# Layer 0's scan: raw tiles in two PSUM banks, the transposes through the two others, a half product between them

## The chip, the cores and the metric

One core of one Trainium2 chip runs the whole model as one program. The metric is the device time of that program in microseconds. The program is written in single instructions: TensorE (PE) multiplies and writes to PSUM only, VectorE (DVE), ScalarE (ACT) and GpSimd (POOL) do everything between products, SyncE (SP) starts the loads of the weights. All data are fp32.

## The reference, cut to what matters

The model is a first transformer block and a second block of two layers. The change is in the second block's layer 0, in the part that is a Mamba-2 scan over 512 tokens (256 of the context, 256 of the latent). Each layer projects the normed input, sends part of the result (x, B and C) through a five-tap depthwise convolution and a SiLU, scans in both directions in chunks of 128 tokens, and gates the sum with a SiLU of z:

```
def dwconv_silu(x, w, bias):                       # kw = 5
    y = lax.conv_general_dilated(x, w[:, None, :], window_strides=(1,), padding=[(kw // 2, kw // 2)], ...)
    return jax.nn.silu(y + bias)

# ssd_chunked, per chunk of 128 tokens and group g of 8, 4 heads of 64 in each
chunk_states = jnp.einsum('bclgn,bclgr,bclgrp->bcgrpn', bc, decay_to_end, xc)
h = h * chunk_decay + chunk_states                 # from chunk to chunk
cb = jnp.einsum('bclgn,bcsgn->bclsg', cc, bc)
y = (jnp.einsum('bclsg,bclsgr,bcsgrp->bclgrp', cb, lmat, xc)
     + jnp.einsum('bclgn,bcgrpn,bclgr->bclgrp', cc, h_in, jnp.exp(cs)))

y = (yf + yb + ssd_d[:, None] * xs)
ssd = rmsnorm(y * jax.nn.silu(z), ssd_norm_g) @ w_ssd_o
```

The projections that feed it, `h @ w_in` (x, B, C and z of all eight groups) and the gate `gs`, are computed in the same stage.

## The kernel before, in words

The scan of layer 0 goes through eight groups `g`. Two kinds of work are interleaved by hand in it.

The first kind is the scan of group g. Its four convolved tiles (x in two, B, C; 128 channels by 512 tokens each) lie in `CV`. PE transposes the two x tiles and the B tile, four 128x128 transposes each (line 1512), ScalarE copies them out (`turned`, line 2031), PE makes the products C by B (line 1521, "the CB product"), which VectorE masks twice into `CBM` (line 2784). POOL scales x by its weights (`XD`, line 3165); PE makes from it and the transposed B the change of the state (line 1536, "the delta"); VectorE carries the state on (lines 2800 to 2806); PE multiplies the state by C (line 1553) and VectorE takes that to `Y` (lines 2826 to 2829). This goes three steps, i = 0, 1, 2. Then come four units: ScalarE makes decays (lines 2070, 2074), VectorE masks them (line 2839, `masked`), PE multiplies (line 1570, `within`). At the end VectorE adds all to Y (lines 2845 and 2851, `sum_y`), and one group later it multiplies by the gated z (line 2860, `times_z`).

The second kind is the projection of group g+1's x, B, C and of group g's z: one chunk of weights each (1024x256), three chunks to a group, `m = 3g, 3g+1, 3g+2`. Each chunk is multiplied by Winograd's form of the 2x2 block product, which takes seven half-size products (`pe_scan`, n = 0 to 6, each four matmuls of 256 columns, line 629; the trace counts each fp32 matmul twice) in place of eight. POOL prepares sums of the weights (lines 673 to 681). ScalarE keeps one product (`act_scan`, line 685). VectorE assembles the four results out of the banks PB (`dve_scan`, lines 693 to 705: U2, c11, U4, U3, c2, c21). PE may begin chunk m+1 only when VectorE has done U4 (line 697) of chunk m: this is the wait on `scan_free` in `pe_scan` for n = 0.

The assembled tiles of a chunk ("raw tiles", two of 128x512) go to `RAW_H`, an unused part of H in SBUF. ScalarE reads them for the middle tap and the bias (line 1990, `middle`), VectorE reads them for the four other taps (`raw_taps`, line 2738; source `RAW_H`, destination and second input the CV buffer in SBUF), and ScalarE reads z's raw tiles for the SiLU (line 2093). The CV buffer of layer 0 shows as X in the trace. In group 0 and in layer 1 the taps read a product straight from the PSUM banks PB instead (line 2771).

Of PSUM's eight banks four (PB) hold the seven products. The other four are PA[0], PA[1] (x tiles' transposes, then delta and the state's product, then `within`), PS[:,0] (B's transposes) and PS[:,1] (the CB product).

The order on PE is written by hand. `SCAN_FILL` says how many of the 21 half products go into each slot of a group: before, 2 behind the CB product, 2, 3, 2 behind the deltas of i = 0, 1, 2, then 2, 3, 2, 3 ahead of the four `within`, and 2 at the end. PE waits for `s_y` (the adds of `sum_y`) of the group before, at the head of a group. VectorE's order within a group: assemble(3g-1), the two masks of CB, times_z(g-1), the states of i = 0 and 1, assemble(3g), the rest of the states, masked(0), taps of tile 0, masked(1), taps of tile 1, assemble(3g+1), masked(2), taps of tile 2, masked(3), taps of tile 3, sum_y.

Of the kernel before, what the change touches and what calls it, by code (L numbers as in the profile page):

```python
# [9 lines left out]
P = 128  # L10
D = 1024
KT = D // P
T1 = 256
TT = 512
# [179 lines left out]
SCAN_EARLY = 4  # L194


SCAN_FILL = list(itertools.accumulate((2, 2, 3, 2, 2, 3, 2, 3, 2), initial=0))
assert SCAN_FILL[-1] == 21 and N_SCAN == 3 * SSD_GROUPS + 2


# [12 lines left out]
def program(nc, xT, stream, params, rows, consts, rel_bias, rev_hot, w_dt, scratch, cs_rows, x_kept, mrg_kept, out):  # L213
    ctx = ExitStack()
    with ctx:
# [732 lines left out]
        at += 1024  # L948
        assert at <= ARENA, at
        YT = [area(L_SSD + 2048 * i, 8, T1) for i in (2, 0, 3, 1)]  # L950
        RAW_H = H[:, 0:KT:2, T1:TT]
        SCAN_SUMS = [area(4096, 2, 4, 4, P), area(L_MRG, 2, 4, 4, P)]
        SCAN_KEEP, SCAN_U3 = par[:, 0:T1], c_("c_before")
        SCAN_U2, SCAN_U4 = (wdt[:, 0, 4 * i:4 * i + 4, :].rearrange("p k n -> p (k n)") for i in range(2))
# [123 lines left out]
        def _(pe):  # L1078
# [257 lines left out]
            for la in range(DEPTH_2):  # L1336
# [163 lines left out]
                def scan_group(g):  # L1500
                    b = g % 2
                    tok = [t for t in range(4) if live(la, t)]
                    if g >= 1:

                        pe.wait_ge(sem("s_y"), LAYER["s_y"] * la + 2 * g)
                    for i, bank in enumerate((PA[0], PA[1], PS[:, 0])):
                        if i == 2 and g == 0:
                            pe.wait_ge(sem("cs_turned"), la + 1)

                        pe.wait_ge(sem("s_conv"), LAYER["s_conv"] * la + 4 * g + i + 1)  # L1510
                        for t in range(4):
                            mm = pe.transpose(bank[:, t * P:(t + 1) * P], CV[b][:, i, t * P:(t + 1) * P], ident)
                        mm.then_inc(sem("s_turns"), 1)
                    pe.wait_ge(sem("s_conv"), LAYER["s_conv"] * la + 4 * g + 4)
                    if g == 0:

                        pe.wait_ge(sem("dt_rest"), LAYER["dt_rest"] * la + 2)
                    else:
                        pe.wait_ge(sem("s_cbm"), LAYER["s_cbm"] * la + 2 * g)
                    for t in tok:  # L1520
                        mm = pe.matmul(PS[:, 1, t * P:(t + 1) * P], CV[b][:, 2, t * P:(t + 1) * P],
                                       CV[b][:, 3, t * P:(t + 1) * P], start=True, stop=True)
                    mm.then_inc(sem("s_cb"), 1)
                    if la == 0:
                        fill(g, 0)
                    else:
                        project(g + 1, (0,))
                        if g + 1 == SSD_GROUPS:
                            project_z(g, (0,))

                    pe.wait_ge(sem("s_turned"), LAYER["s_turned"] * la + 3 * g + 3)
                    for i in range(3):
                        for d, order in enumerate((F_ORDER, B_ORDER)):
                            n = 6 * g + 2 * i + d
                            pe.wait_ge(sem("s_xd"), LAYER["s_xd"] * la + n + 1)
                            pe.matmul(PA[0][:, 256 * d:256 * d + 256], BT[:, order[i], :], XD[d],  # L1536
                                      start=True, stop=True).then_inc(sem("s_delta"), 1)
                        if la == 0:
                            fill(g, i + 1)
                        else:  # L1540
                            project(g + 1, ((1,), (2, 3), (4,))[i])
                            if g + 1 == SSD_GROUPS and i + 1 < T // P:
                                project_z(g, (i + 1,))

                        if i and inter_count(la, g, i - 1):
                            pe.wait_ge(sem("s_inter_read"), LAYER["s_inter_read"] * la + inter_count(la, g, i - 1))
                        for d, order in enumerate((F_ORDER, B_ORDER)):
                            n = 6 * g + 2 * i + d
                            pe.wait_ge(sem("s_state"), LAYER["s_state"] * la + n + 1)
                            t = order[i + 1]  # L1550
                            if live(la, t):
                                for q in range(2):
                                    mm = pe.matmul(PA[1][:, 256 * d + P * q:256 * d + P * q + P],  # L1553
                                                   HT[d][:, P * q:P * q + P], CV[b][:, 3, t * P:(t + 1) * P],
                                                   start=True, stop=True)
                                mm.then_inc(sem("s_inter"), 1)
# [17 lines left out]

                    if la == 0:
                        for u in range(len(units)):
                            fill(g, 4 + u)
                            within(u)
                        fill(g, 8)
                        return  # L1580
                    z_tiles = ((), (), (), (0,), (1,))
                    if g + 1 == SSD_GROUPS:
# [121 lines left out]
        def _(act):  # L1704
# [189 lines left out]
            for la in range(DEPTH_2):  # L1894
# [86 lines left out]
                def middle(g, chunks):  # L1981
                    b = g % 2
                    if la == 0 and 0 < g < SSD_GROUPS:
                        for j in chunks:
                            act.wait_ge(sem("scan_free"), 3 * (3 * (g - 1) + j) + 3)
                            if g >= 2 and j == 0:
                                act.wait_ge(sem("s_y"), 2 * (g - 1))
                            for t in range(2):
                                i, ch = 2 * j + t, channels(g, 2 * j + t)
                                copy(CV[b][:, i, :].rearrange("p (a n) -> p a n", a=2), RAW_H[:, 2 * t:2 * t + 2, :],  # L1990
                                     ACT.Identity, scale=par[:, W0 + 2 * 32 + ch:W0 + 2 * 32 + ch + 1],
                                     bias=par[:, CBs + ch:CBs + ch + 1]).then_inc(sem("s_mid"), 1)
                        return
                    for j in chunks if g < SSD_GROUPS else ():
# [24 lines left out]
                            act.wait_ge(evacuated[pair], 2 * before + i % 2 + 1)  # L2019
                        copy(CV[b][:, i, 0:Tc], CV[b][:, i, 0:Tc], ACT.Silu).then_inc(sem("s_conv"), 1)  # L2020

                def turned(g):

                    for i, bank in enumerate((PA[0], PA[1], PS[:, 0])):
                        act.wait_ge(sem("s_turns"), LAYER["s_turns"] * la + 3 * g + i + 1)
                        src = bank.rearrange("p (t n) -> p t n", t=4)
                        if i == 0 and g >= 1:

                            act.wait_ge(sem("s_xc"), LAYER["s_xc"] * la + 2 * len(units) * g)
                        dst = BT[:, :, :] if i == 2 else XG[:, :, i * P:(i + 1) * P]  # L2030
                        copy(dst, src, ACT.Copy).then_inc(sem("s_turned"), 1)  # L2031
# [55 lines left out]
                def silu_z(g):  # L2087
                    if la == 0:
# [1 line left out]
                        if g >= 1:  # L2090
                            act.wait_ge(sem("s_sum"), g)
                        for i in range(2):
                            copy(ZT[:, i, :].rearrange("p (a n) -> p a n", a=2), RAW_H[:, 2 * i:2 * i + 2, :], ACT.Silu)\
                                .then_inc(sem("s_silu"), 1)
                        return
                    pair, _ = GROUPS[f"z{la}"][g]
                    act.wait_ge(chunk_done, CHUNKS[f"z{la}"][g] + 1)
# [29 lines left out]
                if la == 0:  # L2127
# [1 line left out]
                        act.wait_ge(evacuated[pair], 2 * before + 2)  # L2129
                    act.dma_start(mrg_kept, MRG).then_inc(sem("kept_saved"), 16)  # L2130
                    for g in range(SSD_GROUPS):
                        turned(g)
                        if g:
                            silu_z(g - 1)
                        row_exps(g)
                        act_scan(act, 3 * g)
                        decay_exps(g, 0)
# [31 lines left out]
                def gates(j):  # L2169
                    if la == 0:  # L2170
                        act.wait_ge(sem("scan_free"), 3 * (N_SCAN - 4 + j) + 3)
                        for t in range(2):
                            gate = GS[:, 2 * j + t, :]
                            copy(gate.rearrange("p (a n) -> p a n", a=2),
                                 gate.rearrange("p (a n) -> p a n", a=2) if j else RAW_H[:, 2 * t:2 * t + 2, :],
                                 ACT.Sigmoid).then_inc(sem("gs_open"), 1)
                        return
                    pair, _ = GROUPS[f"gs{la}"][j]
                    act.wait_ge(chunk_done, CHUNKS[f"gs{la}"][j] + 1)
# [101 lines left out]
        def _(v):  # L2281
# [319 lines left out]
            for la in range(DEPTH_2):  # L2601
# [125 lines left out]
                def raw_taps(g, tiles):  # L2727


                    for i in tiles:  # L2730
                        v.wait_ge(sem("s_mid"), 4 * g + i + 1)
                        ch = channels(g, i)
                        for tap in (0, 1, 3, 4):
                            s_ = tap - 2
                            lo, hi = max(0, -s_), T1 - max(0, s_)
                            dst = CV[g % 2][:, i, :].rearrange("p (a b) -> p a b", a=2)[:, :, lo:hi]
                            src = RAW_H[:, 2 * (i % 2):2 * (i % 2) + 2, lo + s_:hi + s_]
                            ins = vec.scalar_tensor_tensor(dst, src, par[:, W0 + 32 * tap + ch:W0 + 32 * tap + ch + 1],  # L2738
                                                           dst, ALU.mult, ALU.add)
                            if tap == 4:  # L2740
# [4 lines left out]
                def assemble(m):  # L2745


                    tiles = RAW_H
                    if m >= N_SCAN - 3:
                        j = m - (N_SCAN - 4)  # L2750
                        tiles = GS[:, 2 * j:2 * j + 2, :].rearrange("p t (a n) -> p (t a) n", a=2)
                    dve_scan(v, m, tiles[:, 0, :], tiles[:, 1:4:2, :], tiles[:, 2, :])

                def taps(g, tiles):

# [22 lines left out]
                def states(g):  # L2778
                    if la == 0 and g >= 1:
                        assemble(3 * g - 1)  # L2780
                    v.wait_ge(sem("s_cb"), LAYER["s_cb"] * la + g + 1)
                    for d, tri in enumerate((c_("tri_le"), c_("tri_ge"))):
                        n = T // P
                        vec.tensor_tensor(CBM[:, d, tok, :], PS[:, 1, 0:T].rearrange("p (a b) -> p a b", a=n),
                                          tri.unsqueeze(1).broadcast_to([P, n, P]), ALU.mult)\
                            .then_inc(sem("s_cbm"), 1)
                    if g >= 1:
                        times_z(g - 1)
                    for i in range(3):
                        for d, order in enumerate((F_ORDER, B_ORDER)):  # L2790
# [562 lines left out]
```

## Time and profile before

| | us |
|---|---|
| median of three runs | 3018.41 |
| their lowest and highest | 3017.31, 3023.1 |
| the profiled execution's own time | 3029.04 |
| its span (first to last instruction) | 3027.2 |
| PE busy in it | 2938.1 (97%) |
| DVE busy | 1484.5 (49%) |
| ACT busy | 814.8 (27%) |
| POOL busy | 1036.3 (34%) |
| layer 0's scan, from its first transposes to its last `within` products | from 1121.3 to about 1540 of the span |

A row of the time line gives the start, the time from the first start to the last end of the instructions merged in it, the engine, the line, the operation, output and inputs, and how many (x); in brackets the idle time ahead of it and what ended that. A row by source line gives the shortest, median and longest duration in ns and the first and last start. DVE, at half the span busy, is only of interest where PE waits for it.

### The profile page before, as it was taken

Reading aid. Unit: us, or ns where it says so; the run is one execution under the profiler, and the core shown is the slowest. Engines: PE = TensorE matmul, PEld = TensorE weight load, DVE = VectorE, ACT = ScalarE, POOL = GpSimd, SP = SyncE. Lnnn points to the kernel's source line nnn. Section 1 sums busy time; section 2 is a strip of 40 time slices with the busy share of each in tenths; the row PEclk is TensorE's granted clock in tenths of the full one; section 3 lists DMA queues with packets and bytes.
Section 4 is the critical chain, followed back from the end, with each engine's and each line's share of the span. In section 5 each row is a group of like instructions: output and inputs, shape, how many; then the busy total and the mean of one; then the engine's idle time right before and its main releaser. Section 6 shows DMA issues by size and latency. Waiting matters only on the chain.

```text
span 3027.2 us, 40501 instructions
## 1 busy us (share of the span) xinstructions
PE 2938.1 (97%) x16088; PEld 2400.4 (79%) x16088; DVE 1484.5 (49%) x2765; ACT 814.8 (27%) x1778; POOL 1036.3 (34%) x876
## 2 busy tenths in 40 slices
PE   8999999999999999999999999999998999999999
PEld 7776799998855558887878788888886666678998
DVE  1243267813265638888763533342237555541651
ACT  1022222201022325665630110110104355540210
POOL 0000234574400115565654334443230111110686
PEclk9999999999999899999999999999999999999999
DMA  7455434442356033222232122222331323334443
GB/s 258 147 205 205 153 140 155 165 167 86 124 196 222 29 127 112 98 98 98 98 125 84 70 84 85 96 84 84 112 112 42 118 99 111 106 111 153 154 168 112
DMA packets 68977, 377.63 MB, mean 125 GB/s; under 512 B 6378, under 2 KB 24874, under 8 KB 26304
## 3 DMA queue, kind: packets, MB, share of 16 engines
q1 hardware_dynamic: 49120, 334.60, 30.6%
q10 hardware_dynamic: 18704, 36.90, 3.6%
q0 software_dynamic: 976, 3.63, 0.3%
q8 instruction: 127, 2.08, 0.3%
q14 instruction: 50, 0.41, 0.0%
HBM read 366.50 MB, written 4.42 MB: 123 GB/s over the span
## 4 chain that ended last, share of the span: by engine, by line
PE 60%; DVE 7%; ACT 1%; issue 1%; PEld 1%; POOL 0%; PEldq 0%; POOLq 0%; ACTq 0%; DVEq 0%
PE PB L501 12%; PE PB L629 8%; PE PA L501 7%; PE PB L1481 7%; PE PS L501 6%; PE PB L381 5%; PE PB L1188 2%; DVE X L2738 2%; PE PB L1454 2%; PE PB L425 2%; PE PA L1536 1%; PE PA L1570 1%; PE PA L1553 1%; ACT work L1945 1%; PE PB L1495 1%
## 5 line engine op out<-in xcount | busy, mean ns | idle before, releaser
L536 POOL TENSOR_TENSOR sums<-ring 128x512 f32<-128x512 f32 x115 | 150.6, 1309 | 603.4 <-PE PA L501 246.8
L501 PE MATMUL PB<-work,sums 128*128 128x128 f32 (+1 forms) x1360 | 230.5, 327 | 0.0
L1481 PE MATMUL PB<-H,ring 128*128 128x512 f32 (+1 forms) x576 | 229.5, 547 | 0.0
L501 PEld LDWEIGHTS PB<-work,sums 128*128 128x128 f32 x1360 | 207.0, 191 | 17.6
L501 PE MATMUL PA<-work,sums 128*128 128x128 f32 (+1 forms) x1280 | 208.9, 318 | 0.0
L734 DVE TENSOR_TENSOR work<-PA,work 128x128 f32<-128x128 f32 (+1 forms) x53 | 18.9, 357 | 381.4 <-ACT work L718 381.4
L501 PEld LDWEIGHTS PA<-work,sums 128*128 128x128 f32 x1280 | 187.4, 191 | 13.6
L3165 POOL TENSOR_TENSOR work<-work 128x256 f32<-128x256 f32 x96 | 59.7, 643 | 402.6 <-ACT work L2031 343.3
L1481 PEld LDWEIGHTS PB<-H,ring 128*128 128x128 f32 x576 | 109.0, 191 | 96.6 <-issue 92.2
L1188 PE MATMUL PB<-H,ring 128*128 128x256 f32 (+1 forms) x640 | 175.0, 428 | 0.4 <-DVE rstd L2381 0.2
L734 DVE TENSOR_TENSOR work<-PB,work 128x256 f32<-128x256 f32 (+1 forms) x34 | 13.0, 382 | 320.8 <-ACT work L718 320.8
L1188 PEld LDWEIGHTS PB<-H,ring 128*128 128x128 f32 x640 | 120.1, 192 | 46.3 <-issue 33.0
L541 POOL TENSOR_TENSOR sums<-ring,sums 128x512 f32<-128x512 f32 x115 | 151.9, 1321 | 9.0
L381 PE MATMUL PB<-work,ring 128*128 128x256 f32 (+1 forms) x544 | 152.7, 442 | 0.7 <-DVE work L2771 0.7
L539 POOL TENSOR_TENSOR sums<-sums,ring 128x512 f32<-128x512 f32 x115 | 149.6, 1301 | 0.0
L537 POOL TENSOR_TENSOR sums<-ring 128x512 f32<-128x512 f32 x115 | 149.0, 1296 | 0.0
L718 ACT ACTIVATE work<-PS 128x128 f32<-128x128 f32 (+1 forms) x53 | 17.5, 330 | 480.8 <-PE PA L501 433.8
L501 PE MATMUL PB<-work,ring 128*128 128x128 f32 (+1 forms) x840 | 143.5, 325 | 0.0
L629 PE MATMUL PB<-work 128*128 128x256 f32 x624 | 143.2, 382 | 0.0
L381 PEld LDWEIGHTS PB<-work,ring 128*128 128x128 f32 x544 | 103.2, 190 | 48.6 <-issue 38.4
L501 PEld LDWEIGHTS PB<-work,ring 128*128 128x128 f32 x840 | 127.0, 191 | 10.4
L501 PE MATMUL PS<-work,ring 128*128 128x128 f32 (+1 forms) x760 | 133.7, 319 | 0.0
(440 smaller groups left out, 6054.2 us busy)
## 6 DMA issues: line engine op xcount, KB each, us to landing
ring<-stream SPq DMA_DIRECT2D x314, 1024.0 KB, 4.8
sums<-cs_rows ACTq DMA_DIRECT2D x16, 1024.0 KB, 4.7
sums<-cs_rows ACTq DMA_DIRECT2D x16, 512.0 KB, 3.7
work<-work ACTq DMA_DIRECT2D x16, 256.0 KB, 4.8
work<-scratch POOLq DMA_DIRECT2D x1, 2560.0 KB, 14.0
mrg_kept<-work ACTq DMA_DIRECT2D x1, 2048.0 KB, 11.3
work<-mrg_kept ACTq DMA_DIRECT2D x1, 2048.0 KB, 10.7
X<-xT SPq DMA_DIRECT2D x2, 512.0 KB, 5.7
```

The costliest lines, as they stand in the source:

```text
L381: mm = pe.matmul(PB[:, pair, t, 0:T], ring[:, c % SLOTS, k, t * P:(t + 1) * P], rhs(k), start=(k == 0), stop=(k == KT - 1))
L425: mm = pe.matmul(PB[:, pair, t, 0:T], ring[:, c % SLOTS, k, t * P:(t + 1) * P], rhs(KT * part + k), start=(part == 0 and k == 0), stop=(pa ...
L501: mm = pe.matmul(fast_bank(side, bank)[:, col:col + width], weight(k), right(4 * part + k), start=first and opens and k == 0, stop=last an ...
L536: nc.gpsimd.tensor_tensor(su[:, 0], a21, a22, ALU.add).then_inc(sem("w_summed"), 1)
L537: nc.gpsimd.tensor_tensor(su[:, 2], a11, a21, ALU.subtract).then_inc(sem("w_summed"), 1)
L539: nc.gpsimd.tensor_tensor(su[:, 1], su[:, 0], a11, ALU.subtract).then_inc(sem("w_summed"), 1)
L541: nc.gpsimd.tensor_tensor(su[:, 3], a12, su[:, 1], ALU.subtract).then_inc(sem("w_summed"), 1)
L629: mm = pe.matmul(fast_bank(0, bank)[:, col:col + T1], weight(k), right(k), start=opens and k == 0, stop=k == 3, skip_group_check=True)
L1188: mm = pe.matmul(PB[:, pair, t, 0:T], ring[:, c % SLOTS, k, t * P:(t + 1) * P], H[:, k, 0:T], start=(k == 0), stop=(k == KT - 1))
L1454: mm = pe.matmul(PB[:, pair, t, 0:T], ring[:, c % SLOTS, k, t * P:(t + 1) * P], H[:, k, 0:T], start=(k == 0), stop=(k == KT - 1))
L1481: mm = pe.matmul(PB[:, pair, t, 0:Tc], ring[:, c % SLOTS, k, t * P:(t + 1) * P], H[:, k, 0:Tc], start=(k == 0), stop=(k == KT - 1))
L2738: ins = vec.scalar_tensor_tensor(dst, src, par[:, W0 + 32 * tap + ch:W0 + 32 * tap + ch + 1], dst, ALU.mult, ALU.add)
```

## The change

Six things change, all of them in layer 0's scan only (`la == 0`); layer 1 runs as it did.

1. The raw tiles are assembled into PSUM, `PS[:, 0]` and `PS[:, 1]`, in place of `RAW_H`. ScalarE's middle tap, VectorE's four other taps, the SiLU of z and the first gate read them there.
2. The transposes of the B tile go through PA[0] in place of PS[:,0], and the CB product goes to PA[1] in place of PS[:,1].
3. So PE transposes the two x tiles, does the first half product of chunk 3g (n = 0), waits until PA[0] is copied out, transposes B, waits until PA[1] is copied out, makes the CB product, then does n = 1. From there the slots are as they were.
4. PE waits for both masks of CB (`s_cbm`) ahead of the state's product of i = 0, which writes PA[1]. The wait for the masks of the group before, ahead of the CB product, goes.
5. ScalarE copies B's transposes out behind the SiLU of the z of group g-1, no longer ahead of it.
6. VectorE does times_z(g-1) ahead of the wait for the CB product, no longer behind the masks.

```diff
-SCAN_FILL = list(itertools.accumulate((2, 2, 3, 2, 2, 3, 2, 3, 2), initial=0))
+SCAN_FILL = list(itertools.accumulate((1, 1, 2, 3, 2, 2, 3, 2, 3, 2), initial=0))
-        RAW_H = H[:, 0:KT:2, T1:TT]
...
-                    for i, bank in enumerate((PA[0], PA[1], PS[:, 0])):
+                    for i, bank in enumerate((PA[0], PA[1], PS[:, 0] if la else PA[0])):
+                        if i == 2 and la == 0:
+                            fill(g, 0)
+                            pe.wait_ge(sem("s_turned"), 3 * g + 1)
...
-                    else:
+                    elif la:
                         pe.wait_ge(sem("s_cbm"), LAYER["s_cbm"] * la + 2 * g)
+                    if la == 0:
+                        pe.wait_ge(sem("s_turned"), 3 * g + 2)
                     for t in tok:
-                        mm = pe.matmul(PS[:, 1, t * P:(t + 1) * P], CV[b][:, 2, t * P:(t + 1) * P],
+                        mm = pe.matmul((PS[:, 1] if la else PA[1])[:, t * P:(t + 1) * P], CV[b][:, 2, t * P:(t + 1) * P],
...
-                        fill(g, 0)
+                        fill(g, 1)
...
+                        if i == 0 and la == 0:
+                            pe.wait_ge(sem("s_cbm"), 2 * g + 2)
...
-                                copy(CV[b][:, i, :].rearrange("p (a n) -> p a n", a=2), RAW_H[:, 2 * t:2 * t + 2, :],
-                                     ACT.Identity, scale=par[:, W0 + 2 * 32 + ch:W0 + 2 * 32 + ch + 1],
+                                copy(CV[b][:, i, :], PS[:, t, :], ACT.Identity,
+                                     scale=par[:, W0 + 2 * 32 + ch:W0 + 2 * 32 + ch + 1],
...
-                        turned(g)
+                        turned(g, (0, 1))
                         if g:
                             silu_z(g - 1)
+                        turned(g, (2,))
...
-                            src = RAW_H[:, 2 * (i % 2):2 * (i % 2) + 2, lo + s_:hi + s_]
+                            src = PS[:, i % 2, :].rearrange("p (a b) -> p a b", a=2)[:, :, lo + s_:hi + s_]
...
-                    tiles = RAW_H
-                    if m >= N_SCAN - 3:
-                        j = m - (N_SCAN - 4)
-                        tiles = GS[:, 2 * j:2 * j + 2, :].rearrange("p t (a n) -> p (t a) n", a=2)
-                    dve_scan(v, m, tiles[:, 0, :], tiles[:, 1:4:2, :], tiles[:, 2, :])
+                    j = m - (N_SCAN - 4)
+                    tiles = GS[:, 2 * j:2 * j + 2, :] if j > 0 else PS[:, :, :]
+                    dve_scan(v, m, tiles[:, 0, 0:T1], tiles[:, :, T1:TT], tiles[:, 1, 0:T1])
...
                     if la == 0 and g >= 1:
                         assemble(3 * g - 1)
+                        times_z(g - 1)
...
-                        vec.tensor_tensor(CBM[:, d, tok, :], PS[:, 1, 0:T].rearrange("p (a b) -> p a b", a=n),
+                        vec.tensor_tensor(CBM[:, d, tok, :], (PS[:, 1] if la else PA[1])[:, 0:T].rearrange("p (a b) -> p a b", a=n),
...
-                    if g >= 1:
+                    if la and g >= 1:
                         times_z(g - 1)
```

## Rows read from the trace of the kernel before

**Rows 1.** PE's waits over the whole span: total us, times, longest us.
```profile
PE PB L629 <- DVE wdt L697: 24.7, 8, 3.4
```
**Rows 2.** Time line of PE: head of group 0, head and end of group 7.
```profile
1121.28 1.06 PE L1512 MATMUL PA<-con,X 128*128 128x128 f32 x8 [1.58 <-DVE work L2879]
...
1491.51 1.04 PE L1512 MATMUL PA<-con,X 128*128 128x128 f32 x8
...
1540.13 3.62 PE L629 MATMUL PB<-H,ring 128*128 128x256 f32 x16
```
**Rows 3.** Time line of PE: first two half products of chunk 3g+2, seven groups.
```profile
1157.07 3.69 PE L629 MATMUL PB<-H,ring 128*128 128x256 f32 x16 [1.70 <-DVE wdt L697]
...
1208.81 5.38 PE L629 MATMUL PB<-H,ring 128*128 128x256 f32 x16 [2.71 <-DVE wdt L697]
...
1262.57 6.35 PE L629 MATMUL PB<-H,ring 128*128 128x256 f32 x16 [3.42 <-DVE wdt L697]
...
1317.30 3.69 PE L629 MATMUL PB<-H,ring 128*128 128x256 f32 x16 [3.41 <-DVE wdt L697]
...
1369.38 5.38 PE L629 MATMUL PB<-H,ring 128*128 128x256 f32 x16 [3.41 <-DVE wdt L697]
...
1475.22 5.38 PE L629 MATMUL PB<-H,ring 128*128 128x256 f32 x16 [3.41 <-DVE wdt L697]
...
1525.50 3.72 PE L629 MATMUL PB<-H,ring 128*128 128x256 f32 x16
```
**Rows 4.** Stretches: us, busy PE, PEld, DVE, ACT, POOL (x), PEclk, DMA share, GB/s.
```profile
1371.00:1373.00 2.00, 2.00 (x6) 1.55 (x6) 2.00 (x2) 2.00 (x6) 1.92 (x2) 0.50 0.00 0
```
**Rows 5.** Time line of DVE in group 4, up to U4 of chunk 3g+1, and after it.
```profile
1349.91 0.76 DVE L2826 TENSOR_TENSOR work<-PA,work 128x256 f32<-128x256 f32 x2 [0.22 <-PE PA L1553]
...
1357.87 3.32 DVE L2738 SCALAR_TENSOR_TENSOR X<-H,par,X 128x508 f32<-128x508 f32 x4
...
1361.12 1.63 DVE L2839 TENSOR_TENSOR work<-work 128x1024 f32<-128x1024 f32 x1
...
1362.67 5.57 DVE L2738 SCALAR_TENSOR_TENSOR X<-H,par,X 128x508 f32<-128x508 f32 x4
...
1368.83 0.41 DVE L697 TENSOR_TENSOR wdt<-PB,wdt 128x256 f32<-128x256 f32 x1
...
1377.65 3.09 DVE L2738 SCALAR_TENSOR_TENSOR X<-H,par,X 128x508 f32<-128x508 f32 x4
```
**Rows 6.** Time line of POOL beside the taps of tile 1.
```profile
1361.63 2.25 POOL L678 TENSOR_TENSOR work<-work,ring 128x512 f32<-128x512 f32 x1
```
**Rows 7.** By source line, DVE: durations ns min/median/max, first and last start.
```profile
L2738 DVE SCALAR_TENSOR_TENSOR X<-H,par,X x112: 733/751/1760, 1146.1 to 1485.8; 128x508 f32<-128x508 f32 x56, 128x510 f32<-128x510 f32 x56
...
L2771 DVE SCALAR_TENSOR_TENSOR X<-PB,par,X x16: 739/748/749, 1056.4 to 1075.9; 128x508 f32<-128x508 f32 x8, 128x510 f32<-128x510 f32 x8
...
L701 DVE TENSOR_TENSOR H<-PB,wdt x23: 673/680/683, 1138.0 to 1524.2; 128x512 f32<-128x512 f32 x23
```
**Rows 8.** Time line of all engines at the head of group 4.
```profile
1331.90 0.42 DVE L697 TENSOR_TENSOR wdt<-PB,wdt 128x256 f32<-128x256 f32 x1
1331.91 1.04 PE L1512 MATMUL PA<-con,X 128*128 128x128 f32 x8
...
1332.55 1.08 ACT L2031 ACTIVATE work<-PA 128x512 f32<-128x512 f32 x2 [3.21 <-PE PA L1512]
...
1333.99 1.16 ACT L2093 ACTIVATE work<-H 128x512 f32<-128x512 f32 x2
...
1335.52 1.68 DVE L2860 TENSOR_TENSOR work<-work 128x1024 f32<-128x1024 f32 x1
...
1336.47 5.11 ACT L2056 ACTIVATE work<-sums 64x256 f32<-64x256 f32 x12
...
1337.57 1.03 PE L1536 MATMUL PA<-work 128*128 128x256 f32 x4
```
**Rows 9.** Time line of DVE at the end of group 4: adds of sum_y.
```profile
1382.30 1.28 DVE L2851 TENSOR_TENSOR work<-work,PA 128x512 f32<-128x512 f32 x2 [0.23 <-PE PA L1570]
```

More of the change, by code:

```diff
@@ L1538, in scan_group @@
                         if la == 0:
-                            fill(g, i + 1)
+                            fill(g, i + 2)
                         else:
@@ L1576, in scan_group @@
                         for u in range(len(units)):
-                            fill(g, 4 + u)
+                            fill(g, 5 + u)
                             within(u)
-                        fill(g, 8)
+                        fill(g, 9)
                         return
@@ L2020, in silus, with turned @@
                         copy(CV[b][:, i, 0:Tc], CV[b][:, i, 0:Tc], ACT.Silu).then_inc(sem("s_conv"), 1)
-                def turned(g):
-                    for i, bank in enumerate((PA[0], PA[1], PS[:, 0])):
+                def turned(g, tiles=(0, 1, 2)):
+                    for i, bank in enumerate((PA[0], PA[1], PS[:, 0] if la else PA[0])):
+                        if i not in tiles:
+                            continue
                         act.wait_ge(sem("s_turns"), LAYER["s_turns"] * la + 3 * g + i + 1)
@@ L2092, in silu_z @@
                         for i in range(2):
-                            copy(ZT[:, i, :].rearrange("p (a n) -> p a n", a=2), RAW_H[:, 2 * i:2 * i + 2, :], ACT.Silu)\
-                                .then_inc(sem("s_silu"), 1)
+                            copy(ZT[:, i, :], PS[:, i, :], ACT.Silu).then_inc(sem("s_silu"), 1)
                         return
@@ L2173, in gates @@
                             gate = GS[:, 2 * j + t, :]
-                            copy(gate.rearrange("p (a n) -> p a n", a=2),
-                                 gate.rearrange("p (a n) -> p a n", a=2) if j else RAW_H[:, 2 * t:2 * t + 2, :],
-                                 ACT.Sigmoid).then_inc(sem("gs_open"), 1)
+                            copy(gate, gate if j else PS[:, t, :], ACT.Sigmoid).then_inc(sem("gs_open"), 1)
                         return
```

## The prediction

> **What bounds the kernel now.** I read the page first: PE is busy 97% of the span, so only stretches in which PE stands still or runs slowly can give time. The table of PE's waits then names one large wait: half products that wait for VectorE's U4, eight times, 24.7 us in all and 3.4 us at most [rows 1]. The time line of PE places it. Group 0 begins at 1121.28 and group 7 at 1491.51 [rows 2], 370.2 us for seven groups; group 7 itself, which has no wait, ends at 1540.13 and took 48.6 us for the same instructions on PE. Seven such groups are 340.3 us, so 29.9 us are lost. They lie at one place, the first half product of chunk 3g+2, n = 0: waits of 1.70, 2.71, 3.42, 3.41 and 3.41 us in groups 0 to 4 and 3.41 in group 6 [rows 3]; group 5's row, not shown, is like group 3's (3.41). That is 21.5 us. (The eighth wait of [rows 1], the other 3.2 us, comes behind group 7 and is not touched.) Behind four of the seven waits, those of groups 1, 2, 4 and 6, the two half products take 5.38, 6.35, 5.38 and 5.38 us in place of 3.69 [rows 3]: 7.7 us more. There the granted clock is 0.50 of full speed [rows 4], so 1.2 in place of 2.4 GHz, after a pause of 2.7 us or more; groups 0, 3 and 5 show no such drop. 21.5 and 7.7 make 29.2; 0.7 us is small gaps.
>
> Why VectorE is late is on its own time line of group 4 [rows 5]. From 1349.91, when it takes the state's product of i = 1, to the end of U4 at 1369.24 it never pauses: 19.3 us. In it the four taps of tile 0 take 3.32 us and those of tile 1 5.57 us, where the four of tile 3, with POOL quiet, take 3.09. An add of POOL beside tile 1's taps takes 2.25 us [rows 6], against a mean of some 1.3 us for these adds in the page's list of groups: each engine holds up the other. Over the stage the taps from SBUF go from 733 to 1760 ns, median 751 [rows 7]. An instruction of VectorE with one input in PSUM and one in SBUF does not suffer: 23 times line 701, 673 to 683 ns, across the whole stage [rows 7], in which the page's slices show POOL about half busy.
>
> **The change part by part.** *Taps from PSUM (1).* The taps' first input moves to PSUM, the second stays in SBUF. The same tap from PSUM takes 739 to 749 ns [rows 7], though with POOL quiet; with line 701's steadiness I take 0.75 us each, 3.09 for four, with POOL busy too. The bound on the other side is that they stay as slow as now. Ahead of U4 this saves 3.32 - 3.09 = 0.23 and 5.57 - 3.09 = 2.48, together 2.71 us per group. Waits of up to 2.71 us go, 3.41 becomes 0.70. Groups 0 and 1 end near no wait; groups 2 to 6 keep 0.70 each, 3.5 us. Gain in waits 21.5 - 3.5 = 18.0 us. The clock drops come with the long waits: the one of 1.70 had none, and 0.7 us is less. I count all 7.7 us as gained. VectorE's other instructions with two SBUF inputs can still meet POOL; masked(1) takes 1.63 us [rows 5], and shifted against POOL it could take some tenths more or less. I count nothing.
>
> The Trainium skill has a rule that speaks against the move: "VectorE: DVE Perf Modes", the section on the TRN2 errata, gives VectorE 58 cycles of fixed cost from SBUF and 120 from PSUM. As an estimate from that page, 62 cycles at 0.96 GHz are 0.065 us a tap, 0.5 us for the eight ahead of U4, and the gain would be about 22 us in place of 25.7. The trace disagrees: 748 against 751 ns at the medians [rows 7]; so I leave it out.
>
> *Assembling into PSUM (1).* No instruction of VectorE before writes to PSUM. The nearest rows are the same adds into SBUF, 0.41 us for 256 columns (line 697, [rows 5]) and 0.68 for 512 [rows 7]. I take no difference, as reading shows none between the two memories. As bounds: 0.1 us less an add, or twice as long. Twice means +1.5 us for assemble(3g), of which 0.22 falls into VectorE's pause at 1349.91 [rows 5], and +0.4 for c11 ahead of U4 of 3g+1: 1.7 us later, waits of 1.3 to 2.4 us and only some 8 to 14 us gained.
>
> *ScalarE reading PSUM (1).* Two reads of a kind: PSUM to SBUF, 1.08 us for two copies, and the SiLU from SBUF, 1.16 for two [rows 8]. Nothing lost. Its wait for an assembled chunk ends earlier with VectorE.
>
> *The head of a group (2, 3, 5, 6).* Measure from PE's first transpose (1331.91 in group 4's head, [rows 8]). Eight transposes take 0.9 us to the next start; a half product 1.7, the B transposes 0.45, the CB product 0.9. All are the instructions of before, so PE's sum is the same and the first delta stays at +5.7 (1337.57, [rows 8]) if no wait binds. New waits: n = 0 at +0.9 needs U4, which ends at +0.4 (1331.90 + 0.42): it holds by 0.5 us here and by more when the taps are short, since VectorE then waits for PE as at [rows 9]. B's transposes at +2.6 need PA[0] copied: ScalarE starts at +0.64, 0.54 us each, done by +1.2; CB at +3.0 needs PA[1], done by +1.7. B's copy starts when its transposes are done, +3.3, behind the SiLU, which ends at about +2.9 (1335.15 - 1331.91 = 3.2 before, behind a third copy): ready at +3.9 against the delta's +5.7. The row exponentials, at +4.6 before behind a table load (1336.47), start some 0.65 us later, and so do the decays behind them, for which VectorE has no pause in [rows 5]. times_z takes 1.7 us [rows 8] from the SiLU's end at +2.9, the two masks of CB about 1.4 (two of line 701's size), done by +6.0; the state's product that now waits for them comes behind the delta (0.9) and two half products (3.5), at +10. What is queued behind these waits on PE is everything, but each is released 0.5 to 4 us ahead. Cost nothing.
>
> *The end of a group.* From PE's resumption at 1369.38 [rows 3] to sum_y's adds at 1382.30 it is 12.9 us, and there VectorE waits 0.23 us for the last `within` [rows 9]. PE will be 1.7 us quicker there (no clock drop); VectorE is quicker by what POOL costs tile 2's taps, as tile 1's 2.48 us by the same engine's adds. The balance stays, and the half products at a group's end (3.5 us) cover what is off in it.
>
> Sum: 18.0 + 7.7 = 25.7 us. The profiled execution, 3029.0, would be 3003; the three runs' median lies 10.6 us (0.35%) below that execution, and the same gain from 3018.4 is 2992.7, say 2993. At most the full 29.9 us go: 2988.5.
>
> **The rivals.**
> *The drops stay.* The waits shrink but the clock falls elsewhere, or behind the short waits. For it: two of the six waits of 2.7 us or more had no drop, so the wait alone doesn't decide. Against: no drop behind 1.70. Gain 18: 3000.
> *PSUM writes are dear.* As worked out, 3004 to 3010. Nothing speaks for it but that no row excludes it.
> *Nothing moves.* Taps from PSUM are held up by POOL as before, or what they save POOL takes back in masked and the state's adds. 3018. Against: line 701's 673 to 683.
> *Slower.* VectorE pays x more for each access to the raw tiles in PSUM. Ahead of the decisive U4 stand eight taps, three writes of assemble(3g) and one of c11, 12x less 0.22 of pause. From x = 0.24 us it eats the 2.71; at x = 0.4 the waits grow by 1.9 us in seven groups, 13 us: 3031. Against: the equal medians for reads.
>
> The Trainium skill ("SBUF — State Buffer", section "Who interferes with whom") says that of VectorE and GpSimd the one that starts first keeps the shared port for its whole instruction, and that PSUM inputs stay out of it. By it the taps go free, but masked(1) can still land behind a whole add of POOL. The trace agrees in so far as line 701 stays even while line 2738 reaches 1760 ns.
>
> **How the numbers follow.** Main case 0.66 (2987 to 2997); drops stay 0.14; dear writes 0.08; nothing moves 0.07; slower 0.05. The range, 2987 to 3008, holds the first three nearly whole. This kernel's measurement can tell 0.2%, 6 us, from no change: faster 0.88, same 0.07, slower 0.05.
>
> **What would show it.** Line 2738's taps all at 0.74 to 0.76 us; the wait for line 697 under 1 us in groups 1 to 6 and no 5.38 us pair behind it; distance from group 0 to 7 about 344 us; the first delta 5.7 us behind the first transpose; writes to PS of 0.41 and 0.68. I am wrong if the taps still reach over 1 us, if the writes to PS are clearly longer, or if PE's waits show up at the group's head (lines 1512, 1521, 1536).

## The result, and the profile after

The changed kernel takes 2997.3 us at the median of five runs (2996.97 to 3000.34), against 3023.1 (3017.31 to 3030.25) for the kernel before beside it, whose runs spread more. The ratio on record is 0.9927, 95% interval 0.9912 to 0.9941: 0.7% faster (the two medians alone would give 0.9915, as two of the five runs of the kernel before lie at 3030). Forecast were 2993, 2987 to 3008. A second set on another chip gave 2998.89 against 3018.26, ratio 0.9932 (0.9912 to 0.9952).

The profiled execution's own time went from 3029.04 to 3000.34, its span from 3027.2 to 2998.5: 28.7 us. The time line of PE splits them: 5.3 us ahead of the stage, 22.8 in groups 0 to 6, 0.6 behind. The first transposes of groups 0 and 7 and the end of group 7:

```profile
1115.95 1.07 PE L1514 MATMUL PA<-con,X 128*128 128x128 f32 x8 [1.58 <-DVE work L2884]
...
1463.41 1.04 PE L1514 MATMUL PA<-con,X 128*128 128x128 f32 x8
...
1512.04 3.62 PE L629 MATMUL PB<-H,ring 128*128 128x256 f32 x16
```

Groups 0 to 6 now take 1463.41 - 1115.95 = 347.5 us, before 370.2 [rows 2]: 22.8 us. Group 7 takes 48.6, as before. The stage begins 5.3 us earlier, and that is not the change's doing. Ahead of it stand 64 small products for the time steps, untouched by the diff. PE's time line of the kernel before, and of the changed kernel, there:

```profile
1011.05 13.91 PE L1597 MATMUL PS<-wdt,H 128*128 128x64 f32 x64 [0.40 <-ACTq L314]
```

```profile
1013.17 7.36 PE L1603 MATMUL PS<-wdt,H 128*128 128x64 f32 x64 [0.40 <-ACTq L314]
```

They run once at half clock and once at full: the granted clock is 0.50 in the first and 1.00 in the second. That is 6.55 us. The changed kernel begins these products 2.1 us later, which takes as much off, and 0.9 us come between them and the stage. The changed kernel profiled again (below) shows 13.92, and begins its stage at 1121.36. Over the ten profiles of this case the stage begins at 1120.6 to 1121.4 in the four with the slow products (the kernel before and the changed one among them), and at 1112.5 to 1116.2 in the six with the quick ones. It is a draw of each execution: it comes and goes between two profiles of the same kernel.

Inside the stage, the half products of chunk 3g+2 in groups 1 to 4 and 6 of the changed kernel [rows 3]:

```profile
1198.77 3.69 PE L629 MATMUL PB<-H,ring 128*128 128x256 f32 x16
...
1248.78 3.69 PE L629 MATMUL PB<-H,ring 128*128 128x256 f32 x16 [1.34 <-DVE wdt L697]
...
1298.79 3.69 PE L629 MATMUL PB<-H,ring 128*128 128x256 f32 x16 [1.34 <-DVE wdt L697]
...
1348.80 3.69 PE L629 MATMUL PB<-H,ring 128*128 128x256 f32 x16 [1.34 <-DVE wdt L697]
...
1448.81 3.69 PE L629 MATMUL PB<-H,ring 128*128 128x256 f32 x16 [1.34 <-DVE wdt L697]
```

The wait is gone in groups 0 and 1 and 1.34 us in the five others. No pair takes more than 3.69 us, and that of group 0, not shown, takes 3.72: no clock drop is left there. PE's waits over the whole span [rows 1]:

```profile
PE PB L629 <- DVE wdt L697: 9.9, 6, 3.2
```

6.7 us in the groups and the 3.2 behind group 7, which stayed.

Why: the instructions of VectorE by source line, min/median/max ns [rows 7]: the taps, then the assembling adds by destination, PSUM (PS) and, in the last chunks, SBUF (work):

```profile
L2744 DVE SCALAR_TENSOR_TENSOR X<-PS,par,X x112: 732/748/751, 1140.8 to 1458.3; 128x508 f32<-128x508 f32 x56, 128x510 f32<-128x510 f32 x56
...
L701 DVE TENSOR_TENSOR PS<-PB,wdt x23: 685/689/690, 1132.7 to 1496.2; 128x512 f32<-128x512 f32 x23
L701 DVE TENSOR_TENSOR work<-PB,wdt x3: 671/679/679, 1511.8 to 1544.4; 128x512 f32<-128x512 f32 x3
...
L695 DVE TENSOR_TENSOR PS<-PB,par x23: 421/423/423, 1131.7 to 1495.2; 128x256 f32<-128x256 f32 x23
L695 DVE TENSOR_TENSOR work<-PB,par x3: 407/414/415, 1510.9 to 1543.4; 128x256 f32<-128x256 f32 x3
```

The slowest of 112 taps takes 751 ns, before 1760. A write to PSUM costs VectorE 9 to 10 ns more than one to SBUF. VectorE's time line of group 4, the one of [rows 5], from the state's product of i = 1 to U4, with POOL's beside it:

```profile
1331.40 0.76 DVE L2831 TENSOR_TENSOR work<-PA,work 128x256 f32<-128x256 f32 x2 [0.21 <-PE PA L1559]
...
1333.43 1.27 POOL L3150 TENSOR_TENSOR work<-work 128x512 f32<-128x512 f32 x1 [4.60 <-ACT work L2093]
...
1333.85 1.93 DVE L2844 TENSOR_TENSOR work<-work 128x1024 f32<-128x1024 f32 x1
...
1336.61 0.42 DVE L2833 TENSOR_TENSOR work<-PA,work 128x256 f32<-128x256 f32 x1 [0.83 <-PE PA L1559]
...
1337.07 1.36 DVE L2834 TENSOR_TENSOR work<-work 128x256 f32<-128x256 f32 x1
...
1338.79 1.05 DVE L2834 TENSOR_TENSOR work<-work 128x256 f32<-128x256 f32 x1
1339.77 3.08 DVE L2744 SCALAR_TENSOR_TENSOR X<-PS,par,X 128x508 f32<-128x508 f32 x4
...
1342.77 1.89 DVE L2844 TENSOR_TENSOR work<-work 128x1024 f32<-128x1024 f32 x1
...
1344.57 3.08 DVE L2744 SCALAR_TENSOR_TENSOR X<-PS,par,X 128x508 f32<-128x508 f32 x4
...
1348.24 0.41 DVE L697 TENSOR_TENSOR wdt<-PB,wdt 128x256 f32<-128x256 f32 x1
```

From 1331.40 to the end of U4 at 1348.65 it is 17.25 us; it was 19.33. The taps gave 2.7 us, and two instructions that still have two inputs in SBUF took 0.6 to 0.7 back: masked(1) takes 1.89 (before 1.63), and the first of the two adds of line 2834 takes 1.36, where the kernel before has, in group 4:

```profile
1355.58 0.95 DVE L2829 TENSOR_TENSOR work<-work 128x256 f32<-128x256 f32 x1
```

What masked(0) takes doesn't count: VectorE is through with it 0.83 us before PE's product for line 2833 is there. At the head of group 4 PE doesn't wait: its first transposes and its first delta are 5.66 us apart, as before [rows 8]:

```profile
1313.39 1.04 PE L1514 MATMUL PA<-con,X 128*128 128x128 f32 x8
...
1319.05 1.03 PE L1540 MATMUL PA<-work 128*128 128x256 f32 x4
```

### The profile page after: what moved, and what is told of

Same layout as the page of the kernel before. It is cut to its first block, busy times and chain, and to the rows that moved or that the text cites. A ratio compares the mean times of both kernels' runs of the same rounds, so it can differ in the third digit from the quotient of the medians.

```text
span 2998.5 us, 40516 instructions
## 1 busy us (share of the span) xinstructions
PE 2923.9 (98%) x16088; PEld 2388.8 (80%) x16088; DVE 1453.4 (48%) x2765; ACT 814.4 (27%) x1778; POOL 1020.8 (34%) x876
## 4 chain that ended last, share of the span: by engine, by line
PE 61%; DVE 7%; ACT 2%; PEld 1%; issue 1%; POOL 0%; PEldq 0%; POOLq 0%; ACTq 0%; DVEq 0%
PE PB L501 12%; PE PB L629 9%; PE PA L501 7%; PE PB L1480 6%; PE PS L501 6%; PE PB L381 5%; PE PB L1187 2%; PE PB L1453 2%; PE PB L425 2%; PE PA L1540 1%; PE PA L1576 1%; PE PA L1559 1%; DVE work L2871 1%; ACT work L1951 1%; PE PB L1494 1%; DVE small L2670 1%
```

## The experiments

My theory: the taps no longer meet POOL, VectorE's way to U4 of chunk 3g+1 is shorter, and both the wait and the clock drops behind it go. The rival: the new order on PE, ScalarE and VectorE does it. Each experiment is told with its median and its ratio to the kernel before on the same chip. Eight experiments ran, in two sets of four on two chips.

**The order alone, raw tiles in SBUF.**

```diff
-                            src = PS[:, i % 2, :].rearrange("p (a b) -> p a b", a=2)[:, :, lo + s_:hi + s_]
+                            src = RAW_H[:, 2 * (i % 2):2 * (i % 2) + 2, lo + s_:hi + s_]
...  (and RAW_H for the assembled tiles, the middle tap, the SiLU of z and the first gate)
```

> The changed kernel's order on PE, ScalarE and VectorE, but the raw tiles stay in SBUF, so the taps read two inputs there. Theory (the gain is the taps' freedom from POOL): the taps take 3.3 and 5.6 us again, PE waits about 3.4 us at chunk 3g+2 in five groups, group 0 to group 7 takes 360 to 371 us, time 3012 to 3022. Rival (the new order of PE, ScalarE or VectorE brought the gain): waits near 1.3 us, 347 us, time about 2997.

Measured: 3024.16 us, ratio 1.0015 (1.0002 to 1.0029). PE's waits and the time line of PE, one group:

```profile
PE PB L629 <- DVE wdt L697: 26.4, 8, 3.7
```

```profile
1316.65 6.23 PE L629 MATMUL PB<-H,ring 128*128 128x256 f32 x16 [3.73 <-DVE wdt L697]
```

The whole gain is gone, and more: the waits are 3.72 us where the kernel before has 3.41. The order brings nothing; by itself it costs 0.3 us a group. The stage, from the head of group 0 to that of group 7, took 374.7 us, and the time is 2.2 us above what was expected too. The gain comes with the place of the raw tiles.

**Time given back on VectorE.**

```diff
+            for _ in range(5 if m % 3 == 1 and m < 3 * (SSD_GROUPS - 1) else 0):
+                vec.tensor_tensor(c11, fast_bank(0, 0)[:, 0:T1], SCAN_KEEP, ALU.add).then_inc(sem("dve_step"), 1)
+                v.wait_ge(sem("dve_step"), next_step(dve_steps))
             vec.tensor_tensor(c11, fast_bank(0, 0)[:, 0:T1], SCAN_KEEP, ALU.add)
```

> The changed kernel with five extra adds (c11 again, each waited for, about 0.45 us) on VectorE ahead of U4 of chunk 3g+1 in groups 0 to 6: some 2.2 us of VectorE's time given back. Theory (VectorE's way to this U4 is all that sets the time, and a clock drop follows a wait of this length in about half of the cases): waits of 3.3 to 3.6 us, +14 to +15 us from the waits and +3 to +8 us from drops, 3014 to 3021. Rival (the drops have nothing to do with the waits): no drops, +15 us, 3012. Second rival (the time hangs on other things): under +8 us.

Measured: 3021.86 us, ratio 1.0016 (1.0002 to 1.0029). PE's time line, groups 1 to 6 without 5:

```profile
1199.56 3.69 PE L629 MATMUL PB<-H,ring 128*128 128x256 f32 x16 [2.44 <-DVE wdt L700]
...
1251.90 5.38 PE L629 MATMUL PB<-H,ring 128*128 128x256 f32 x16 [3.67 <-DVE wdt L700]
...
1305.93 6.31 PE L629 MATMUL PB<-H,ring 128*128 128x256 f32 x16 [3.68 <-DVE wdt L700]
...
1360.89 3.69 PE L629 MATMUL PB<-H,ring 128*128 128x256 f32 x16 [3.67 <-DVE wdt L700]
...
1467.27 5.38 PE L629 MATMUL PB<-H,ring 128*128 128x256 f32 x16 [3.68 <-DVE wdt L700]
```

2.3 us more on VectorE are 2.3 us more wait (3.67 for 1.34), and the clock drops are back in four of the five groups with 3.67 us. The stage took 371.1 us, 23.6 more than the changed kernel's: 16.0 of wait and 7.7 of slow products. With the taps as quick as ever the kernel is as slow as before; the time is 0.9 us above the range that was expected. This shows that each us on VectorE's way to this U4 is a us of PE's wait there, and that the drops come with the long waits.

**POOL's sums one unit later.**

```diff
-                            for m, steps in (((3 * g + 2, (0, 1)),), ((3 * g + 2, (2, 3)),), ((3 * g + 3, range(4)),))[u - 1]:
+                            for m, steps in ((), ((3 * g + 2, (0, 1)),),
+                                             ((3 * g + 2, (2, 3)), (3 * g + 3, range(4))))[u - 1]:
```

> The changed kernel, with POOL's sums for chunk 3g+2 one unit later each (none behind unit 1, steps 0 and 1 behind unit 2, steps 2 and 3 behind unit 3 ahead of the four for 3g+3). Theory (the 1.34 us that PE still waits are VectorE's remaining instructions with two SBUF inputs, blocked by POOL: lines 2834, 2844): line 2834 falls back to 0.43 us, U4 comes 1.0 to 1.5 us earlier, the wait falls to 0 to 0.4 us, group 0 to 7 takes 341 to 343 us, time 2990 to 2993. Rival: POOL blocks masked(2), masked(3) and sum_y instead, VectorE is late at the group's end and PE waits there: 2997 or more.

Measured: 2991.4 us, ratio 0.9910 (0.9893 to 0.9927). The waits of PE for line 697 are one, the one behind group 7. The stretch from group 0 to group 7 and VectorE's groups in it:

```profile
PE PB L629 <- DVE wdt L697: 3.2, 1, 3.2
```

```profile
1112.50:1452.90 340.40, 340.40 (x2017) 294.53 (x2018) 259.77 (x438) 223.70 (x477) 209.51 (x193) 1.00 0.31 115
```

```profile
L2834 DVE TENSOR_TENSOR work<-work 128x256 f32<-128x256 f32 x14 | 6.0, 426 | 0.5
...
L2850 DVE SCALAR_TENSOR_TENSOR work<-X,par,work 128x512 f32<-128x512 f32 x14 | 15.5, 1146 | 0.0
```

PE is busy 340.40 of 340.40 us, the floor that the prediction had from group 7. Line 2834 is down to a mean of 426 ns (1155 in the changed kernel); the blocking moved to sum_y's line 2850 (1146 ns, 889 in the changed kernel), where PE has work to cover it. The time is as expected.

**The same on the kernel before.** The same edit.

> The kernel before, with POOL's order of the previous run. Theory (blocking by POOL makes VectorE late): lines 2829 and 2839 ahead of U4 are freed, the taps of tile 1 stay blocked; PE's wait falls from 3.4 to about 1.9 us, time some 8 to 15 us below before, 3005 to 3015. Rival (VectorE is late for another reason): within 5 us of before.

Measured: 3018.84 us, ratio 1.0005 (0.9994 to 1.0016). The expected time was missed. PE's waits:

```profile
PE PB L629 <- DVE wdt L697: 15.1, 8, 3.2
...
PE PA L1570 <- DVE work L2839: 7.9, 7, 1.1
PE PA L1512 <- DVE work L2851: 6.4, 7, 0.9
```

The wait for U4 fell as foretold, from 3.41 to 1.70 us, and the clock drops are gone with it. But the taps of tile 2, now beside more of POOL's adds, take 6.79 us for four in group 0 (5.90 before), and PE waits at two new places, for masked (line 2839) and at the next group's head for sum_y (line 2851). The stage took 368.9 us, against 370.2. With the taps in SBUF this order only moved the blocking; it pays once the taps are out of it. Whether another order of POOL would have paid without PSUM wasn't tried.

**The changed kernel again, beside the next three.** No edit.

> The changed kernel unchanged, to stand on the same chip beside the next two. Theory (22.8 us of the profile's 28.7 belong to the change, the other 5 to a clock drop ahead of the stage that the profile of before happened to have): time 2995 to 2998, the stage from group 0 to 7 again 347.5 us, and the 64 small products ahead of it at either 7.4 or 13.9 us by chance. Rival (the change also moves what lies ahead of the stage): always 7.4.

Measured: 2998.89 us, ratio 0.9932; the time is 0.9 us above what was expected. The stage took 1468.80 - 1121.36 = 347.4 us with the same five waits, and the 64 small products took 13.92 us. So the two profiles' 5.3 us ahead of the stage are not the change's. Its six runs go from 2996.76 to 3006.34, two of them at 3006.3; the kernel before's eleven from 3016.2 to 3030.52, two of them above 3030.

**Two of the side moves undone.**

```diff
-                        turned(g, (0, 1))
+                        turned(g)
                         if g:
                             silu_z(g - 1)
-                        turned(g, (2,))
...  (and times_z(g - 1) behind the masks of CB again)
```

> The changed kernel with two of its side moves undone: B's transposes are copied out ahead of the SiLU of z again, and times_z comes behind the masks of CB again. PSUM tiles and PE's order stay. Theory (these moves only shift when POOL's squares meet VectorE): the wait stays between 0.7 and 2.0 us, time within 5 us of the changed kernel. Rival (the moves are what keeps PE supplied at the head): waits at lines 1514, 1525 or 1540, over 5 us slower.

Measured: 2991.29 us, ratio 0.9909 (0.9889 to 0.9929). Both expectations were missed. The undone kernel is 7.6 us quicker than the changed one beside it at the medians, 6.2 in the profiles' stage (341.3 us): PE doesn't wait for U4 in groups 0 to 6 at all. The reason is on its time line of group 4, whose first transposes are at 1310.98:

```profile
1331.44 1.22 DVE L2842 TENSOR_TENSOR work<-work 128x1024 f32<-128x1024 f32 x1
...
1332.00 1.78 POOL L3148 TENSOR_TENSOR work<-work 128x512 f32<-128x512 f32 x1 [5.59 <-ACT work L2093]
...
1334.20 0.42 DVE L2831 TENSOR_TENSOR work<-PA,work 128x256 f32<-128x256 f32 x1 [1.54 <-PE PA L1559]
1334.66 0.76 DVE L2832 TENSOR_TENSOR work<-work 128x256 f32<-128x256 f32 x1
...
1339.75 1.25 DVE L2842 TENSOR_TENSOR work<-work 128x1024 f32<-128x1024 f32 x1
1339.88 2.26 POOL L678 TENSOR_TENSOR work<-work,ring 128x512 f32<-128x512 f32 x1
```

masked(0) starts 20.46 us behind the group's head in both kernels. POOL's first add of squares starts 20.04 us behind it in the changed kernel (1333.43 - 1313.39) and 21.02 here. Changed: POOL is first, masked(0) takes 1.93 us. Here: VectorE is first, masked(0) takes 1.22 and POOL 1.78. These 0.7 us by themselves bring nothing: in both kernels VectorE then waits for PE's product, whose adds start 23.22 us behind the head (1336.61 - 1313.39, 1334.20 - 1310.98). What counts comes behind it, from the same shift of POOL: the first add of line 2832 takes 0.76 (line 2834 in the changed kernel: 1.36), and masked(1), which starts just ahead of POOL here and just behind it there, 1.25 (1.89). Together 1.24 us, of the wait of 1.34.

POOL's squares come behind ScalarE's work. ScalarE's row exponentials start 6.13 us behind the head here, 5.15 in the changed kernel and 4.56 in the kernel before [rows 8]; POOL's squares start at 21.02, 20.04 and 19.45. So the change made POOL 0.6 us later than before, and without the two moves it is later still by one us, and out of VectorE's way. This points to the move on ScalarE. Which of the two did it wasn't tried.

**POOL's sums later, again,** beside the changed kernel on one chip.

> The changed kernel with POOL's sums for chunk 3g+2 one unit later, again, beside the changed kernel itself on one chip. Theory: no wait in groups 0 to 6 (340.4 us), 6 to 7 us under the changed kernel: 2989 to 2992. Rival (the lower time of its first run was the chip's): within 2 us of the changed kernel.

Measured: 2993.6 us, ratio 0.9912 (0.9892 to 0.9932), against the changed kernel's 2998.89: 5.3 us less at the medians, where 6 to 7 were expected, and 1.6 us above the expected time. No wait for U4 in groups 0 to 6, 340.4 us from group 0 to 7, as in its first run. This profile had the 13.9 us draw.

**VectorE's order behind group 7,** on top of POOL's later sums.

```diff
                     turn_y(0, False)
-                    turn_y(1, False)
                     assemble(N_SCAN - 2)
+                    turn_y(1, False)
...
-                for j in range(3):
-                    scale_gates(j)
+                scale_gates(0)
                 if la == 0:
                     assemble(N_SCAN - 1)
                     turn_y(0, True)
                     turn_y(1, True)
+                for j in (1, 2):
+                    scale_gates(j)
```

> The same kernel, with VectorE's order behind group 7 changed: assemble of the last chunk but one between the two first turns of Y, and assemble of the last chunk behind the first scaled gate. Theory (PE's 3.2 us wait there for U4, and the clock drop behind it, come from VectorE's order alone): the wait for line 697 is gone, 3 to 5 us under the kernel with POOL's later sums: 2985 to 2988. Rival (VectorE has too much to do there anyway, the wait moves to Y's turns or the gates): within 1.5 us.

Measured: 2984.4 us (2983.18 to 2987.92), ratio 0.9883 (0.9864 to 0.9901), 9 us under the run without it and 0.6 under the range that was expected. PE's time line behind group 7, first without the edit (from that kernel's first run), then with it:

```profile
1515.37 1.10 PE L1641 MATMUL PA<-work,small 128*128 128x512 f32 x2 [1.60 <-POOL work L3154]
...
1519.65 5.26 PE L629 MATMUL PB<-H,ring 128*128 128x256 f32 x16 [3.18 <-DVE wdt L697]
```

```profile
1519.04 1.09 PE L1641 MATMUL PA<-work,small 128*128 128x512 f32 x2 [1.59 <-POOL work L3155]
1519.97 3.62 PE L629 MATMUL PB<-H,ring 128*128 128x256 f32 x16
```

The wait of 3.2 us and the slow pair behind it (1.6 us longer) are gone, 4.8 us. In the other profile of the kernel without the edit, the one of the same set, that pair takes 6.63 us, 3.0 too much, which makes 6.2; from the head of group 7 to the last instruction the two profiles of that set are 6.3 us apart. Lowest run against lowest it is 6.9 us (2983.18 and 2990.05). The rest to 9 is not accounted for; both sets of runs hold quick and slow draws. It is the fastest kernel of the case, 1.2% under the one before.

## Why the prediction was right, and where it wasn't

- *Place and size of the loss.* Floor of 340.3 us for seven groups: measured 340.4 once the waits were gone. Right.
- *Taps from PSUM at 0.75 us each, with POOL busy.* 732 to 751 ns in 112 of 112. Right. The Trainium skill's dearer fixed cost for PSUM sources ("VectorE: DVE Perf Modes", the section on the TRN2 errata) doesn't show: medians 748 and 751 ns. VectorE's write to PSUM costs 9 to 10 ns, some 0.04 us on the way to U4. The prediction took this term for unknown, as no instruction of VectorE before wrote to PSUM. That is a misreading: the ten of line 2505 did, outside the stage, and their rows would have closed the rival "PSUM writes are dear" beforehand, since the same width into SBUF takes 0.41 us [rows 5]:

```profile
L2505 DVE TENSOR_TENSOR PS<-work,PA x2: 422/426/430, 373.2 to 373.6; 128x256 f32<-128x256 f32 x2
...
L2505 DVE TENSOR_TENSOR PS<-work,PB x2: 422/425/428, 702.0 to 702.3; 128x256 f32<-128x256 f32 x2
```

- *Residue of the wait.* Forecast 0.70 us in five groups, measured 1.34. This is the term that was mis-sized, 3.2 us in all. I had set the shift of VectorE's other two-input instructions against POOL at nothing. On the way to U4 the first add of line 2834 and masked(1) took 0.6 to 0.7 us of the 2.7 back. The prediction had even cited the rule that bears on it. By the Trainium skill's "SBUF — State Buffer", "Who interferes with whom", who starts first keeps the port. The trace agrees: POOL's start 0.4 us ahead of masked(0) or 0.6 behind it is 0.7 us of masked(0)'s length. To use it one has to lay out who comes first. ScalarE's shift, and so POOL's, was in the prediction (0.65 us later; measured 0.6), but not followed to these two instructions.
- *Clock drops, 7.7 us.* All gone: right. The delayed kernel brought them back. That both sums are 7.7 us is luck: three pairs of 5.38 us and one of 6.3 in both, but which waits are followed by a drop differs.
- *Head and end of a group at no cost.* Right for PE: no wait at either. Wrong for what it does elsewhere: the order alone lengthened the wait from 3.41 to 3.72, and without two of the side moves the residue is zero. The forecast took ScalarE's later start for harmless because VectorE doesn't wait for it; POOL's squares do, and they meet VectorE.
- *Sum.* In the stage 25.7 forecast, 22.8 measured; the 3.2 of the residue make the difference, less 0.3. Of the medians, 3018.41 was forecast to become 2993 and became 2997.3, 21.1 us less. The profile's 28.7 us would have flattered: 5.3 of them are a draw. So would the medians of the five runs beside each other, 25.8 us apart, as good as the forecast by luck: the kernel before had two runs at 3030. Lowest run against lowest it is 20.3 us, and 19.4 in the second set, still less than the stage's 22.8; that rest is open.
- *The signs.* Taps, writes to PSUM (0.42 and 0.69 us) and the first delta at 5.7 us came as named. The wait was to be under 1 us and the stage about 344; they are 1.34 and 347.5.
- *Two readings of its own.* The rival of dear writes was worked out as waits of 1.3 to 2.4 us; with 1.0 us saved a group they are 0.7 to 2.4. The mean of 1.3 us for POOL's adds is that of adds of this size in other stages; line 678's own take 1.26 to 2.26 us in this one. Neither changes the sum.
- *Rivals.* "Nothing moves" and "slower" are out by the taps' and the writes' rows; "the drops stay" by the pairs of 3.69 us.

## What to carry to other kernels

When VectorE and GpSimd share the work, list VectorE's instructions with two inputs in SBUF on the path to the wait, and move one input of the longest to PSUM if two banks can be freed: here 0.75 us against up to 1.76. What remains is decided by who starts first, so an edit on a third engine that shifts GpSimd by one us can give or take a third of what the change brought (some 6 to 8 us here); try GpSimd's order together with it. A wait that stops PE for some 3 us cost here two fifths to half as much again in slow products behind it. And compare two profiles stage by stage: ahead of this stage they differ by up to 9 us with nothing changed.

## What the runs showed of the hardware

- *The length of a wait doesn't decide alone whether the clock drops.* At this one place, waits of 2.7 to 3.7 us were followed by half clock (two half products in 5.4 to 6.4 us instead of 3.69, 1.7 to 2.7 us lost) in 13 of 17 cases over three kernels' profiles; waits of 1.33 to 2.44 us in none of 21. Waits of 3.41 us in the kernel before's profile went both ways. Behind group 7, where the same wait lasts 3.19 us, the pair behind it was slow (5.3 to 6.6 us) in all nine profiles that have the wait. What decides is not shown.
- *A drop that comes and goes stands ahead of the stage too*, where TensorE works in short pieces with pauses of 0.4 to 1.2 us: 64 products of 64 columns take 7.36 us at granted clock 1.00 or 13.9 us at 0.50, 6.5 us between one execution of the same kernel and the next.
- *VectorE writes to PSUM* at 423 ns for 256 columns and 689 for 512, to SBUF at 414 and 679, with one input in PSUM.
